# Token-range norms with four-column-group feature sums, and a later combination in the third attention

## What is computed

```
def layer_norm(x, g, b):
    mu = mean(x, -1); var = mean(square(x - mu), -1)
    return (x - mu) * rsqrt(var + LN_EPS) * g + b

# first block, layer i = 0, 1 (context tokens only where need_ctx, that is i = 0)
xl = layer_norm(ALPHA * xl + gt1_l * o_l, ln1_g[i], ln1_b[i])     # ln1_0, ln1_1
h_l = xl * (1.0 + sc2_l) + sh2_l
f_l = conv_ffn(h_l, ...)
xl = layer_norm(ALPHA * xl + gt2_l * f_l, ln2_g[i], ln2_b[i])     # ln2_0, ln2_1

# second block
h = rms_norm_2(x, mix_norm_g)        # mix_norm, of ln2_1's result
x = x + mixed @ w_out
h = rms_norm_2(x, ffn_norm_g)        # ffn_norm
x = x + (silu(f_gate) * f_up) @ ffn_w_down

# diff_attend: the third attention (layer 1, 8 heads, 512 queries, 768 keys)
p = softmax(s, axis=-1)              # s has two maps t = 0, 1 for each head
a = p[:, 0] - lam * p[:, 1]
o = a @ v
o = rms_norm(o, subln_g) * (1.0 - lambda_init)
```

## Time and profile before

| | us |
|---|---|
| median of 3 runs | 3155.65 |
| lowest, highest | 3155.05, 3157.06 |
| the profiled execution | 3155.81 |
| its span | 3154.0 |
| PE busy | 2933.1 (93%) |
| DVE busy | 1569.0 (50%) |
| ACT busy | 952.8 (30%) |
| POOL busy | 203.9 (6%) |
| chain of waits, PE's share | 80% |
| chain of waits, DVE's share | 13% |

### The profile page before, as it was taken

How to read it: one execution, slowest core, us unless ns; L and a number is a source line. 1 busy time by engine, 2 the same in 40 slices (tenths; PEclk the granted TensorE clock), 3 DMA queues, 4 the chain that set the end, 5 groups by cost and what they waited for, 6 DMA issues and landing times.

```text
span 3154.0 us, 38209 instructions
## 1 busy us (share of the span) xinstructions
PE 2933.1 (93%) x15996; PEld 2302.0 (73%) x15996; DVE 1569.0 (50%) x2466; ACT 952.8 (30%) x1441; POOL 203.9 (6%) x136
## 2 busy tenths in 40 slices
PE   7999998999999989989889999778897899989999
PEld 5775786888888867766668888544565588778887
DVE  3464435433233354257555554489976733343333
ACT  2154533222122132145333232310124522232222
POOL 2000000200000002000010000054410000000000
PEclk9999998999999999999999999888877999999999
DMA  6231000232332212100013232111120033223332
GB/s 245 87 110 58 25 27 28 74 115 100 127 112 109 79 49 74 59 29 1 14 61 100 87 116 84 47 58 42 46 81 32 11 97 97 90 74 94 100 95 85
DMA packets 67770, 238.20 MB, mean 76 GB/s; under 512 B 7440, under 2 KB 10640, under 8 KB 66960
## 3 DMA queue, kind: packets, MB, share of 16 engines
q1 hardware_dynamic: 67312, 234.20, 22.7%
q10 hardware_dynamic: 288, 1.57, 0.1%
HBM read 233.64 MB, written 2.10 MB: 75 GB/s over the span
## 4 chain that ended last, share of the span: by engine, by line
PE 80%; DVE 13%; ACT 4%; issue 3%; DMA 1%; POOL 0%; SPq 0%; DVEq 0%; ACTq 0%; POOLq 0%
PE PSA L562 78%; PE PSA L754 1%; ACT Y L1387 1%; DVE Y L1933 1%; DVE WS L1761 1%; DVE stat L1915 1%; DVE Y L2238 1%; DVE Y L1932 1%; DVE Y L2235 1%; DVE Y L2234 1%; DMA Y<-in_early 1%; DVE Y L1834 1%; DVE stat L2319 1%; ACT Y L1634 0%; ACT WS L1304 0%
## 5 line engine op out<-in xcount | busy, mean ns | idle before, releaser
L562 PE MATMUL PSA<-HS,WS 128*128 128x512 f32 (+1 forms) x7104 | 1494.5, 372 | 61.5 <-DVE HS L1781 44.5
L562 PEld LDWEIGHTS PSA<-HS,WS 128*128 128x128 f32 x7104 | 1241.4, 191 | 326.9 <-issue 81.4
L1761 DVE TENSOR_TENSOR WS<-W,WS 128x1024 fp32r<-128x1024 f32 (+2 forms) x358 | 407.7, 1140 | 714.4 <-ACT WS L1304 713.5
L1304 ACT ACTIVATE WS<-W 128x1024 fp32r<-128x1024 f32 (+2 forms) x358 | 351.3, 983 | 1039.2 <-PE PSA L562 688.7
L562 PE MATMUL PSA<-YS,WS 128*128 128x512 f32 (+1 forms) x2688 | 562.1, 370 | 3.5 <-DVE YS L2351 3.5
L562 PEld LDWEIGHTS PSA<-YS,WS 128*128 128x128 f32 x2688 | 470.4, 189 | 93.0 <-DVE YS L2351 3.9
L562 PE MATMUL PSA<-Y 128*64 128x128 f32 (+9 forms) x2240 | 348.4, 365 | 64.7 <-DVE Y L2248 39.4
L562 PEld LDWEIGHTS PSA<-Y 128*64 128x64 f32 (+4 forms) x2240 | 202.0, 166 | 171.7 <-issue 91.5
L1287 ACT ACTIVATE Y<-PSA 128x512 f32<-128x512 f32 (+3 forms) x89 | 63.4, 713 | 328.7 <-PE PSA L562 325.3
L1680 POOL TENSOR_SCALAR X<-X 128x768 f32<-128x768 f32 (+1 forms) x32 | 64.5, 2045 | 1373.7 <-DVE HS L1781 1373.7
L562 PE MATMUL PSA<-Y,C 128*128 128x512 f32 (+2 forms) x220 | 102.4, 600 | 22.9 <-ACT Y L1619 7.8
(11 more groups left out here) (250 smaller groups left out, 2228.4 us busy)
## 6 DMA issues: line engine op xcount, KB each, us to landing
W<-in_weights SPq DMA_DIRECT2D x396, 512.0 KB, 3.6
Y<-in_early SPq DMA_DIRECT2D x4, 2048.0 KB, 19.6
W<-in_weights SPq DMA_DIRECT2D x24, 256.0 KB, 2.9
X<-in_x SPq DMA_DIRECT2D x4, 768.0 KB, 20.9
W<-in_weights SPq DMA_DIRECT2D x24, 128.0 KB, 2.4
Y<-in_ssm ACTq DMA_DIRECT2D x1, 1024.0 KB, 6.5
out<-X SPq DMA_DIRECT2D x1, 1024.0 KB, 4.8
C<-in_consts SPq DMA_DIRECT2D x1, 948.5 KB, 31.9
```

The lines of the kernel that those rows point to most:

```text
L562: return pe.matmul(out, lhsT, rhs, start=first, stop=last)
L1304: act.activation(WS[:, n % R_RING, 0, 0:f], W[:, c % W_RING, 0:f], ACT.Copy)\
L1761: tt(WS[:, n % R_RING, 1, 0:f], W[:, c % W_RING, 0:f], WS[:, n % R_RING, 0, 0:f].bitcast(F32), ALU.subtract).then_inc(weights_split, 1)
```

## The change

**Norms by token range.** The tokens are split into two ranges: latent and context (512 and 256) for `ln1_0` and `ln2_0`, two halves of 256 (`HALVES`) for the others. The projection ahead of a norm runs its last four tiles (all eight for `mix0`) in two passes, first for range 0, then for range 1, and the steps of range 0's norm stand in the second pass (`two_passes`: a table names tile and feature block at which each is issued). Those of range 1 stand in the first three tiles of the next projection (`first_tiles_of`), which run range 0 to the end and then range 1. `mix0` to `mix2` use other PSUM places there. The split weights that are needed twice, and two chunks of the next projection, get places of their own outside the ring (`HOMES`).

**Sums in column groups.** A sum over features is made with 32 instead of 128 columns of weights, four matmuls at a time, each for a quarter of the range and with its own 32 output partitions (`grouped`, `column_sums`). The root and the reciprocal are then taken over a quarter as many columns (128 or 64), and `spread` brings mean and inverse back to all partitions with four broadcasting matmuls.

**Fewer passes.** Gain, bias and modulation are folded into one scale and one shift per feature (`LN_SCALE`, `LN_SHIFT`), applied by ACT; DVE only multiplies by the inverse. POOL applies gain, bias and ALPHA to `X` (`scale_normed`), for 512 tokens after `ln2_0`. `mix_norm`'s sum of squares is put together from weighted sums of `ln2_1`'s squares and centred values, without squaring the result.

**Third attention.** Scores have a fixed PSUM slot for each map, DVE's work on unit n-1 comes after the maxima of unit n, transposes are those of unit n-2 and outputs those of n-3. The combination uses p0 + p1 * ratio alone; the inverse sum of map 0 is left out, and the head's RMS epsilon is scaled to match. An output gathers in PSUM for a whole head and is copied once. The broadcasting matmuls at the end stand between the first tiles of `mix1`. Rotations in the projection before it stand three tiles later instead of one.

```diff
+HALVES = ((0, S // 2, 0), (S // 2, S // 2, 0))
...
+        PASSES = {key: range(0 if key == "ln1_0" else 4, KD)
+                  for key in ("ln1_0", "ln2_0", "ln1_1", "ln2_1", "ffn_norm")}
...
+                for r, (lo, n, _) in enumerate(rngs):
+                    for k in range(KD):
+                        pe.wait_ge(input_ready, value("input_ready", (name, r, k)))
+                        for (key, chunk), w in zip(jobs, ws):
+                            ins = products(PS[slot(key)][:, lo:lo + n], (w[:, 0, k], w[:, 1, k]),
+                                           (src[:, 0, k, lo:lo + n], src[:, 1, k, lo:lo + n]),
+                                           k == 0, k == KD - 1)
...
+                        if r == 0:
+                            between(k)
...
+            def grouped(out, weights, src, q, k):
+
+                for g in range(4):
+                    ins = mm(out[32 * g:32 * g + 32, :], weights, src[:, g * q:(g + 1) * q], k == 0, k == KD - 1)
+                return ins
...
+            def column_sums(key, what, r, ks):
...
+                    if what == "mean":
+                        tile_ = made_by(key, r, k)
+                        pe.wait_ge(psum_drained[slot(tile_)], turn(tile_))
+                        src = X[:, k, lo:lo + n]
+                    else:
+                        pe.wait_ge(squared, value("squared", (key, r, k)))
+                        src = SQUARES[key][r][:, k, :]
+                    ins = grouped(PS[5][:, 256 * r:256 * r + q], const("m1024")[:, 0:32], src, q, k)
+                    if k == KD - 1:
+                        ins.then_inc(psum_filled[5], 1)
+                    if key == "ln2_1" and what == "var":
+                        if k == 0:
+                            fixed((key, "mix", r), 8)
+                        grouped(PS[8][:, 0:q], LN_SCALE[:, k, 0:1].broadcast_to((P, 32)), src, q, k)
+                if key == "ln2_1" and what == "var" and KD - 1 in ks:
+                    for k in range(KD):
+                        ins = grouped(PS[8][:, q:2 * q], LN_SHIFT[:, k, 0:1].broadcast_to((P, 32)),
+                                      X[:, k, lo:lo + n], q, k)
+                    ins.then_inc(psum_filled[8], 1)
...
+            def spread(key, what, r):
...
+                for g in range(4):
+                    ins = mm(PS[at][:, g * q:(g + 1) * q], const("ident")[:, 32 * g:32 * g + 1].broadcast_to((P, P)),
+                             src[:, 0:q], True, True)
+                ins.then_inc(psum_filled[at], 1)
...
+            def two_passes(key, run, first, then):
+
+                ms = PASSES[key]
...
+                for m in ms:
+                    run(m, 0, None)
...
+                    column_sums(key, lead, 0, range(done, m - 1))
+                    done = max(done, m - 1)
...
+                for j, m in enumerate(ms):
+                    run(m, 1, lambda k: statistic(0, first.get((j, k))))
+                return lambda k: statistic(1, then.get(k))
...
+            def mix0_tile(m, r, between):
+                tile(("mix0", r, m), ("mix0", m), HT2, ALL[r:r + 1], release=r == 1 and m < 3, at=m % 3,
+                     between=between)
+
+            feed_forward(0, ALL, two_passes(
+                "ln1_0", mix0_tile, {(0, 3): "first", (1, 1): "mean", (3, 0): "var0", (3, 4): "var1", (4, 2): "inverse"},
+                {0: "first", 1: "mean", 5: "var", 7: "inverse"}))
...
+            context_stats = two_passes(
+                "ln2_0", down_range(0), {(0, 3): "first", (0, 9): "mean", (2, 1): "var0", (2, 6): "var1",
+                                         (3, 2): "inverse"}, {0: "first", 1: "mean", 5: "var", 7: "inverse"})
...
+            for n in range(len(units) + 5):
+                if n < len(units):
+                    diff_scores(units[n], n)
+                if 2 <= n < len(units) + 2:
+                    diff_transposes(units[n - 2], n - 2)
+                if 3 <= n < len(units) + 3:
+                    diff_output(units[n - 3], n - 3)
+                if head_at(n, 8) is not None:
+                    head_sum(head_at(n, 8))
...
+            head_inverse(0)
+            head_inverse(1)
+            first_tiles([(("mix1", m), ("mix1", m)) for m in range(3)], "head", HS2, LAT,
+                        lambda k: head_inverse(k + 2) if k + 2 < DIFF_H else None)
...
+            feed_forward(1, LAT, two_passes(
+                "ln1_1", mix1_tile, {(0, 3): "first", (0, 6): "mean", (2, 0): "var0", (2, 3): "var1", (2, 7): "inverse"},
+                {0: "first", 2: "mean", 6: "var", 7: "inverse"}))
```

The steps of ACT and DVE for a norm, of POOL, and of DVE in the third attention:

```diff
+                def root_of(r):
+                    q = ranges[r][1] // 4
+                    act.wait_ge(psum_filled[5], turn((key, "var", r)))
+                    act.activation(ROOTS[n_all][:, 0:q], PS[5][:, 256 * r:256 * r + q], ACT.Sqrt,
+                                   bias=eps[:, 1:2] if pre else eps[:, 0:1]).then_inc(psum_drained[5], 1)
...
+                        else:
+                            if k >= 3:
+                                act.wait_ge(input_ready, value("input_ready", (name, r, k - 3)))
+                            act.activation(HTMP[:, k % 3, lo:lo + n], X[:, k, lo:lo + n], ACT.Identity,
+                                           scale=LN_SCALE[:, k, s:s + 1], bias=LN_SHIFT[:, k, s:s + 1])\
+                                .then_inc(input_scaled, one("input_scaled", (name, r, k)))
+                    if k:
+                        if r == 0:
+                            last = made_by(key, 1, HOME_FREE[key](k - 1))
...
+            def scale_normed(layer_key, k_key, n):
+
+                for r in range(2):
+                    pool.wait_ge(input_ready, value("input_ready", (layer_key, r, KD - 1)))
+                for k in range(KD):
+                    ins = pool.tensor_scalar(X[:, k, 0:n], X[:, k, 0:n], SKIP_SCALE[:, k:k + 1],
+                                             SKIP_SHIFT[:, k:k + 1], ALU.mult, ALU.add)
+                ins.then_inc(residual_scaled, one("residual_scaled", k_key))
...
+                def inverse(r):
+                    q = ranges[r][1] // 4
+                    root = ROOTS[n_all][:, 0:q]
+                    dve.wait_ge(psum_drained[5], turn((key, "var", r)))
+                    dve.reciprocal(root, root).then_inc(inverted, one("inverted", (key, r)))
...
+                def norm(r, k):
...
+                        ins = stt(HTMP[:, k % 3, lo:lo + n], x, par("ffn_g", k, 1), ps, ALU.mult, ALU.mult)
+                    else:
+                        ins = tt(x, x, ps, ALU.mult)
...
+            for n in range(len(units) + 6):
+                if head_at(n, 7) is not None:
+                    keep_head(head_at(n, 7))
+                if head_at(n, 9) is not None:
+                    head_variance(head_at(n, 9))
...
+                if 1 <= n <= len(units):
+                    u = units[n - 1]
...
+                    _, s0, s1, inverse, ratio = diff_stat(n - 1)
+                    p0, p1 = P0D[:, (n - 1) % 3, :], P1D[:, (n - 1) % 2, :]
+                    link(dve.reciprocal(inverse, s1))
+                    link(stt(ratio, inverse, stat[:, 36:37], s0, ALU.mult, ALU.mult))
+                    stt(p0, p1, ratio, p0, ALU.mult, ALU.add).then_inc(rows_normalised, one("rows_normalised", u))
```

885 lines of the change are left out of this document (581 added, 304 removed).

## The result

| kernel | median of runs | ratio to before, 95% interval | profiled execution, span |
|---|---|---|---|
| before | 3156.4 us (3155.1 to 3158.0) | 1 | 3155.81, 3154.0 |
| changed | 3085.2 us (3079.9 to 3092.2) | 0.9775 [0.9757, 0.9794] | 3092.22, 3090.4 |
| changed, once more | 3085.1 us (3083.1 to 3087.0) | 0.9768 [0.9752, 0.9785] | 3084.40, 3082.6 |

The change gives 71 us where 114 were forecast. The time lies 2 us above the range of 3012 to 3083. The sign holds, and so do the price of the short matmuls and the period of the third attention. 43 us are missing, and the largest single part of them is in TensorE's waits around the new norms, which the sum put too low.

What follows compares the result with a forecast made beforehand. TensorE, holding 80% of the chain of waits, was taken as the bound. Norms giving 81.6 us and the third attention 32.4 us brought 3155.81 to 3041.8, forecast 3042 us, range 3012 to 3083.

Steps and rivals of the forecast that it cites:

- The sign: Whole kernel: the change makes it faster, given 0.95, against 0.02 for the same and 0.03 for slower.
- the price of the short matmuls: Projection tiles split into halves: a 256-column matmul costs 0.127 us, a tile of 48 takes 6.12 us, 0.66 more.
- the period of the third attention: Third attention: a unit falls from 5.06 us to 4.26 by formula, taken as 4.2; 31 periods take 130.2 us.
- The cheaper price: Rival, half tiles: 256-column matmuls cost 0.115 us, so halves cost nothing and the time is 3029; chance 0.13.
- the loads as a bound: Rival, half tiles: weight loads bound each 256-column matmul at 0.191 us, + 68 us to 3110; chance 0.04.
- the slower rival: Rival: weight loads of 256-column matmuls are not hidden, 0.298 us each, + 246 us to 3288; chance 0.03.
- Sums too dear, spreads too cheap: Norms, 64-column ranges: 0.24 us per set of four sum matmuls, 1.9 a sum; 0.44 us per spread.
- Waits: TensorE's waits around the five new norms: 15.5 us in all, ends 0 and 31, range 0 mostly hidden.
- The chains-do-not-fit rival: Rival, norms: TensorE waits in second passes and before range 1 for + 31 us more, 3073; chance 0.13.
- that rival: Third attention: both maps' scores run one behind the other, 5.0 us a unit, 3067; chance 0.17.
- The tail: End of the third attention, from the last unit's scores to the first mix1 tile: 16.5 us.
- Broadcasts among the tiles: Head end, among the mix1 tiles: six broadcasts of 1.1 us each, 6.6 us, no waits between them.

Runs made afterwards that it cites:

- the fastest kernel: Changed kernel with reordered head end and ln2_0 context range, rotations one tile behind, weight chunks before range 1's root, lambda exponentials earlier: 3049.1 us, ratio 0.9662 to before.
- The filler run: Changed kernel with unused 256-column matmuls put into seven of TensorE's waits: 3095.6 us, ratio 0.9793 to the kernel before.
- the order run: Changed kernel with third-attention units reordered, TensorE's transposes of unit n-2 standing between the scores of map 0 and map 1: 3122.5 us, ratio 0.9889 to before.
- the bank: Changed kernel with ln2_0's context range reordered: two weight chunks ahead of the root, all eight inverse multiplications before the first rest: 3081.1 us, ratio 0.9743 to before.
- the chunks: Changed kernel with the two weight chunks inside range 1's steps made ahead of its root, in all five norms: 3071.9 us, ratio 0.9729 to before.
- the head end: Changed kernel with VectorE making the rest of block h-1 ahead of scaling block h, at the third attention's end: 3076.3 us, ratio 0.9731 to before.
- the rotations: Changed kernel with dq and dk tiles rotated one tile behind again instead of three: 3082.0 us, ratio 0.9748 to before.
- the first maxima: Changed kernel with the lambda exponentials and three small VectorE steps moved from before the first maxima to the start of the dv tiles: 3084.0 us, ratio 0.9765 to before.

## Why the prediction was right or wrong

**256-column matmuls, right.** A half tile in the changed kernel:

```profile
1544.70 3.14 PE L645 MATMUL PSA<-HS,YS 128*128 128x256 f32 x24
1547.77 0.32 PE L645 MATMUL PSA<-X,C 128*32 128x64 f32 x8
```

(1547.77 - 1544.70) / 24 = 0.128 us, against 0.127. The cheaper price, the loads as a bound and the slower rival fall with it. What I had at no cost, the order of `mix0` and of the first four `down` tiles, is not quite free: a 512-column matmul takes 5.67 / 24 = 0.236 us by itself there (`mix0` 3, from 453.99 to its sums at 459.66; 0.235 in the `down` tiles) and 0.223 in a pair with a 256-column one, some 3 us in these nine tiles. Why, no run tells.

**Sums too dear, spreads too cheap.** Ranges of 64 columns, summed and spread:

```profile
515.41 1.10 PE L645 MATMUL PSA<-X,C 128*32 128x64 f32 x64
516.44 2.33 PE L645 MATMUL PSA<-HS,WS 128*128 128x512 f32 x9
518.61 1.00 PE L645 MATMUL PSA<-Y,C 128*128 128x64 f32 x8
519.42 8.44 PE L645 MATMUL PSA<-HS,WS 128*128 128x512 f32 x36
```

Eight sets take 1.03 us, 0.13 a set, below the lower end of 0.16; I had 0.24. A spread takes 0.81 us for 64 columns as for 128; I had 0.44. Its eight records each load full weights, and eight times the 0.115 us of the earlier trace rows would have been the price: the columns are not what it is made of. A set that stands alone between two tiles takes 0.25 us. Some -13 us over the eighteen 64-column sums, -1 over the four of 128 columns and +6 over the sixteen spreads: together 8 us in the change's favour. That is luck, and it hid a part of the misses below.

**Waits, the step that failed.** I gave 15.5 us, with 31 as the end. They are 36: in `ln1_0` 4.5, in `ln2_0` 16 (11.2 of it one wait that I put at 4 and on the wrong thing), in `ln1_1` 4.7, in `ln2_1` 8.0, in `ffn_norm` 3.3. The chains-do-not-fit rival had the direction; I gave it 0.13. Its reason, eight hand-overs, was not the right one. Of the 21 us too few, 10 are at range 1, and the runs put these on a PSUM slot and on weight chunks in the chain. The other 10 are at range 0, which I had hidden but for 2 us: it waits 12.5 us in the five norms, and 12.4 still in the fastest kernel. Two of its waits, 3.02 us in `ln2_0` and 2.91 in `ffn_norm`, can be read. In `ln2_0` VectorE has the rest of block 0 ready at 1127.56, but TensorE's next tiles also need the PSUM slot of the last tile, and the addition that empties it (L2169) stands in VectorE's list behind multiplications and rests of further blocks. TensorE starts 0.31 us after its end:

```profile
1126.87 0.69 DVE L2238 TENSOR_TENSOR HS<-Y,HS 128x512 fp32r<-128x512 f32 x1 [0.98 <-ACT HS L1618]
...
1128.71 0.48 DVE L2169 SCALAR_TENSOR_TENSOR X<-PSA,MOD,X 128x256 f32<-128x256 f32 x1
```
```profile
1129.50 3.88 PE L645 MATMUL PSA<-HS,WS 128*128 128x512 f32 x9 [3.02 <-DVE HS L2238]
```

The profile names the rest, and the addition came later. In `ffn_norm` TensorE likewise starts 0.32 us after that addition. The filler run agrees: there the filler, which needs the slot and no input, starts 0.36 us after the addition. No run moved it.

**What a wait costs, left out.** I had noted that the old norms ran in part at 1.2 GHz and then priced the new waits by their length. Records behind some of them run low: 9 matmuls in 3.8 us and not 2.2 after the waits of 3.0 us (at 1129.50) and 1.5 us (at 1501.86), `dq` 3 at 7.5, two rounds of the attention at 5.0 and not 3.6, the 72 matmuls of `ln2_1` at 11.1 and not 8.8. Each is 1.5 to 2.5 us, some 10 us in all, an estimate from these rows; only those at `dq` 3, in `ln2_1` and in the first units stand beside a kernel in which they are gone.

**Third attention, mechanism right, ends wrong.** The period was forecast by the formula at 4.26, taken as 4.2, and is 4.27. The scores overlap, so that rival falls; the order run shows its price, 37 us and not 25. 31 periods took 133.3 us and not 130.2, 2 of the 3 us in the first four (19.0, where four steady ones are 17.1). The tail, from the scores of the last unit at 1481.26 to the first `mix1` tile, took 20.6 us and not 16.5, 1.7 of it in the first two broadcasts at the low clock. That makes the 7.2 us by which this stretch misses.

**Broadcasts among the tiles, wrong.** I counted 1.1 us each (they are 1.05) and did not follow who waits for what VectorE does between them: 6 x 1.44 us, and 1.53 ahead of them, nearly all of it an order of two instructions (1.1 us are left).

**Costed at nothing.** POOL, the loads, the folded scales and the constant are hidden: no wait names them. The later rotations are not: 3 us.

**The missing 43 us.** The version with all repairs is at 3049, 36 of them back. The repairs are the bank, the chunks, the head end, the rotations and the first maxima. The last 7 are argued only. TensorE's waits around the norms are still 22.7 us in that version, 7 above the 15.5 forecast, and 12.4 of them are those of range 0. The nine tiles at 0.236 us (3 us), the ends of the attention and what still runs at the low clock come on top, and the 8 us of cheap sums stand against them.

## What to carry to other kernels

When statistics or broadcasts are laid between tiles, write down for each engine the list around them and look for the instruction that another engine waits for behind one that it does not need; most of the missing gain was in such orders and cost nothing to take back. A buffer that shares its bank with the next tile's is a wait from its last reader, whatever else is ready. The releaser that a profile names for a wait need not be the one that ended it: compare the start behind the wait with the ends of everything that the engine's list asks for there. And a wait on TensorE can cost 1.5 to 2.5 us more than its length, in work at the lower clock behind it; whether it does, its length did not tell here, so it belongs in the range and not in the sum.

## What the runs showed of the hardware

- Matmuls on different halves of the array's rows ran at once when they stood next to each other in TensorE's list, and not with six transposes between them: 8 records in 1.57 us, 4 alone in 1.55, and 3.1 for both when parted.
- When they overlap, taking work away can undo the overlap: 0.67 us less of other matmuls a unit moved the period by 0.34.
- A spread by four matmuls with one broadcast column as weights takes 0.81 us for 64 and for 128 columns; a set of four 32-column sums takes 0.13 us for 64 columns in a row of eight sets, and 0.25 alone between two tiles; for 128 columns it takes 0.36 us alone.
- The same wait of 1.77, 2.03 or 2.93 us is followed by the low clock in one kernel and not in another. It can fall behind the wait and not in it (1.00 in 2.87 us of wait, 0.76 in the tile behind).
